# Feed-forward: the hidden chunks turned in 32x32 blocks by VectorE and a trip through device memory instead of by TensorE

## The reference, cut to what matters

```python
D_MODEL = 1024; SEQ = 256; DEPTH = 4
FFN_HIDDEN = -(-8 * D_MODEL // (3 * 256)) * 256        # 2816

def swiglu(h, w_gate, w_up, w_down):
    return (jax.nn.silu(h @ w_gate) * (h @ w_up)) @ w_down

for i in range(DEPTH):
    ...                                                # mixer
    f = swiglu(rms_norm(x, norm_gains[i, 2]), ffn_w_gate[i], ffn_w_up[i], ffn_w_down[i])
    x = x + rms_norm(f, norm_gains[i, 3])
```

## Time and profile before

| | us |
|---|---|
| median of three executions | 1390.9 |
| span of the profiled execution, first to last instruction | 1388.9 |
| TensorE busy in the span | 1368.8 |
| VectorE busy | 996.3 |
| ScalarE busy | 793.3 |
| GpSimd busy | 177.8 |
| DMA queue of SyncE, share of 16 engines' span | 48.4% |
| granted TensorE clock over the span | 1.000 |

### The profile page before, as it was taken

The page is one execution under the profiler, slowest core; times in us unless marked ns, Lnnn a source line. Parts: engine busy times, 40 slices in busy tenths (PEclk is TensorE's granted clock), DMA queues, the critical chain, the costliest instruction groups (busy, mean ns, idle before and its releaser), DMA issues.

```text
span 1388.9 us, 20395 instructions
## 1 busy us (share of the span) xinstructions
PE 1368.8 (99%) x6833; PEld 1117.6 (80%) x6833; DVE 996.3 (72%) x1889; ACT 793.3 (57%) x1556; POOL 177.8 (13%) x323
## 2 busy tenths in 40 slices
PE   7999999999999999999999999999999999999998
PEld 6888888887887888889888888888888888877667
DVE  6978655559566755569766555599888666789976
ACT  6676644547665645548656554467665445675344
POOL 4100000000111000002000000001049992000000
PEclk9999999999999999999999999999999999999999
DMA  8534655555423755553336555545356556353132
GB/s 290 167 113 142 231 181 183 189 187 187 146 96 113 248 181 188 193 181 120 122 96 223 187 194 193 182 141 178 122 175 212 181 182 207 126 182 122 61 121 92
DMA packets 154389, 230.35 MB, mean 166 GB/s; under 512 B 7512, under 2 KB 103328, under 8 KB 154320
## 3 DMA queue, kind: packets, MB, share of 16 engines
q1 hardware_dynamic: 152352, 224.05, 48.4%
q0 software_dynamic: 1968, 5.43, 1.4%
HBM read 228.40 MB, written 1.05 MB: 165 GB/s over the span
## 4 chain that ended last, share of the span: by engine, by line
PE 90%; DVE 6%; ACT 2%; issue 1%; DMA 0%; SPq 0%; DVEq 0%; ACTq 0%
PE ps L2050 23%; PE ps L2052 23%; PE ps L2051 23%; PE ps L2056 3%; PE ps L2064 3%; PE ps L2060 3%; PE ps L2980 1%; DVE w_rest L1348 1%; PE ps L2328 1%; PE ps L2387 1%; DVE x L1411 1%; PE ps L2080 1%; ACT w_head L817 1%; PE ps L2894 1%; PE ps L2316 1%
## 5 line engine op out<-in xcount | busy, mean ns | idle before, releaser
L2050 PE MATMUL ps<-w_head,xt_head 128*128 128x512 f32 (+1 forms) x1200 | 471.4, 393 | 4.3 <-DVE w_rest L1348 2.5
L1348 DVE SCALAR_TENSOR_TENSOR w_rest<-w_raw,gain_t,w_head 128x512 fp32r<-128x512 f32 (+1 forms) x596 | 415.4, 757 | 74.7 <-ACT w_head L817 73.8
L817 ACT ACTIVATE w_head<-w_raw,gain_t 128x512 fp32r<-128x512 f32 (+1 forms) x596 | 375.4, 700 | 154.8 <-PE ps L2052 125.3
L2052 PE MATMUL ps<-w_head,xt_rest 128*128 128x512 f32 (+1 forms) x1200 | 461.1, 384 | 0.0
L2051 PE MATMUL ps<-w_rest,xt_head 128*128 128x512 f32 (+1 forms) x1200 | 460.2, 384 | 0.0
L2050 PEld LDWEIGHTS ps<-w_head,xt_head 128*128 128x128 f32 x1200 | 226.5, 189 | 49.9 <-issue 8.3
L2052 PEld LDWEIGHTS ps<-w_head,xt_rest 128*128 128x128 f32 x1200 | 226.2, 188 | 45.3
L2051 PEld LDWEIGHTS ps<-w_rest,xt_head 128*128 128x128 f32 x1200 | 226.8, 189 | 40.7
L1346 DVE TENSOR_TENSOR w_rest<-w_raw,w_head 128x1024 fp32r<-128x1024 f32 x124 | 153.4, 1275 | 82.2 <-ACT w_head L817 81.7
L817 ACT ACTIVATE w_head<-w_raw 128x1024 fp32r<-128x1024 f32 x124 | 124.7, 1053 | 98.2 <-PE ps L2052 96.8
L2050 PE MATMUL ps<-w_head,ht_head 128*128 128x512 f32 x320 | 124.9, 390 | 0.0
(11 more groups left out here) (493 smaller groups left out, 1543.5 us busy)
## 6 DMA issues: line engine op xcount, KB each, us to landing
w_raw<-in_ffn_w_gate_dram SPq DMA_DIRECT2D x88, 512.0 KB, 3.7
w_raw<-in_ffn_w_up_dram SPq DMA_DIRECT2D x88, 512.0 KB, 4.7
w_raw<-in_ffn_w_down_dram SPq DMA_DIRECT2D x88, 512.0 KB, 4.1
w_raw<-in_a_w_in_dram SPq DMA_DIRECT2D x48, 512.0 KB, 4.7
w_raw<-in_b_w_in_dram SPq DMA_DIRECT2D x24, 512.0 KB, 4.6
w_raw<-in_w_in_dram SPq DMA_DIRECT2D x24, 512.0 KB, 4.4
w_raw<-in_a_w_out_dram SPq DMA_DIRECT2D x16, 512.0 KB, 4.4
w_raw<-in_c_w_in_dram SPq DMA_DIRECT2D x10, 512.0 KB, 4.4
```

Of the source, the lines that this page charges most:

```text
L817: ins = act.activation(w_head[:, s, w], raw(u)[:, w], ACT.Copy, scale=1.0 if by is None else by)
L1348: ins = dve.scalar_tensor_tensor(w_rest[:, s, w], raw(u)[:, w], by, hd, ALU.mult, ALU.subtract)
L2050: pe.matmul(out_, hd, wh, start=first, stop=False)
L2052: return pe.matmul(out_, rt, wh, start=False, stop=last)
```

## The change

Of the eleven chunks of each feed-forward part, chunks 1 to 9 are no longer transposed by TensorE. `hidden` now writes `hid` with the token blocks side by side. VectorE turns all 16 blocks of 32x32 of each 128x128 tile in one instruction (`blocks_turned`) into `hid_blocks`, a part of `q_t`. What remains is to move blocks between the four groups of 32 partitions. SyncE does that with one DMA of 256 KB to a new tensor in device memory (`hidden_out`, 2 KB per partition), and, behind the completion of that, four DMAs of 64 KB back to `hid_there`, a part of `k_t` (`hidden_in`, runs of 512 bytes, 32 partitions each). ScalarE's and VectorE's `hidt` then read `hid_there` in SBUF instead of bank 6. Chunk 0 and chunk 10 are transposed by TensorE as before.

```diff
+BY_DMA = NCH - 2
 ...
+        hid_blocks = q_t[:, 0:2, :].rearrange("p i t -> p (i t)")
+        hid_there = k_t[:, 0:2, :].rearrange("p i t -> p (i t)")
+        hid_way = nc.dram_tensor("hid_way", (P, 2 * TOK), F32).ap()
+        arrived = hid_there.rearrange("p (a g j) -> p g a j", a=4, g=4)
 ...
 # SyncE
+                def hidden_out(c, more=0):
+                    sp.wait_ge(hid_turned, BY_DMA * li + c + more)
+                    sp.dma_start(hid_way[:, :], hid_blocks).then_inc(hid_out, 16)
+
+                def hidden_in(c, more=0):
+                    sp.wait_ge(hid_out, 16 * (BY_DMA * li + c) + more * 16)
+                    for b in range(4):
+                        rows = slice(32 * b, 32 * b + 32)
+                        sp.dma_start(hid_there[rows, :].rearrange("p (a e) -> p a e", a=4),
+                                     hid_way[:, P * b:P * b + P].rearrange("(a i) e -> i a e", a=4)).then_inc(hid_in, 16)
 ...
-                with sp.Fori(0, NCH - 1) as i:
-                    load_gu(u + 2, i * 3, 0, (i + 1) * FCH)
-                    load_gu(u + 3, i * 3, 4, (i + 1) * FCH)
-                    load_down(u + 4, i * 3, i * 2)
+                for i in range(2):
+                    load_gu(u + 2 + 3 * i, 0, 0, (i + 1) * FCH)
+                    load_gu(u + 3 + 3 * i, 0, 4, (i + 1) * FCH)
+                    load_down(u + 4 + 3 * i, 0, 2 * i)
+                with sp.Fori(0, NCH - 3) as i:
+                    load_gu(u + 8, i * 3, 0, (i + 3) * FCH)
+                    hidden_out(1, i)
+                    load_gu(u + 9, i * 3, 4, (i + 3) * FCH)
+                    hidden_in(1, i)
+                    load_down(u + 10, i * 3, i * 2 + 4)
                 u += 2 + 3 * (NCH - 1)
+                hidden_out(BY_DMA)
+                hidden_in(BY_DMA)
                 load_down(u, 0, 2 * (NCH - 1))
 ...
 # ScalarE
-                    act.wait_ge(hidt_ready, f + c + 1 + more)
-                    act.activation(ht_head[:, :, :], ps[:, 6, :].rearrange("p (t c) -> p t c", t=2), ACT.Copy).then_inc(hidt_head, 1)
+                def hidt(c, down_before, more=0):
+                    act.wait_ge(unit_used, down_before + 1 + more * 3)
+                    act.wait_ge(hid_in, 64 * (BY_DMA * n["ffn"] + c) + more * 64)
+                    act.activation(in_order(ht_head), arrived, ACT.Copy).then_inc(hidt_head, 1)
 ...
 # VectorE
-                        last = dve.scalar_tensor_tensor(hid[:, m, :], ps[:, bank + m, FCH:2 * FCH], rstd_x[:, m:m + 1], gate_s[:, m, :], ALU.mult, ALU.mult)
+                        up, gated = (t_.rearrange("p (t c) -> p t c", t=2) for t_ in (ps[:, bank + m, FCH:2 * FCH], gate_s[:, m, :]))
+                        last = dve.scalar_tensor_tensor(hid[:, :, P * m:P * m + P], up, rstd_x[:, m:m + 1], gated, ALU.mult, ALU.mult)
 ...
+                def blocks_turned(c, more=0):
+                    dve.wait_ge(hid_done, f + c + 1 + more)
+                    dve.transpose(hid_blocks.rearrange("p (b g j) -> p g b j", b=4, g=4),
+                                  hid.rearrange("p t (m b i) -> p (t m) b i", m=M, b=4)).then_inc(hid_turned, 1)
 ...
+                    dve.tensor_tensor(in_order(ht_rest), arrived, in_order(ht_head).bitcast(F32), ALU.subtract).then_inc(hidt_rest, 1)
 ...
                 hidden(1, bank=4)
+                blocks_turned(1)
                 rest(u + 2 + RING)
 ...
                     rest(u + 5 + RING, i)
                     hidden(2, i)
+                    blocks_turned(2, i)
                     rest(u + 6 + RING, i)
                     rest(u + 7 + RING, i)
                     hidt(2, i)
 ...
 # TensorE
                 down(u + 4, 0, first=True)
-                turn_hidden(1)
                 with pe.Fori(0, NCH - 3) as i:
+                    pe.wait_ge(hid_done, f + 2 + i)
                     gate_up(u + 5, i)
                     down(u + 7, 1, i)
-                    turn_hidden(2, i)
                 u += 2 + 3 * (NCH - 2)
+                pe.wait_ge(hid_done, f + NCH - 1)
                 gate_up(u)
                 two_last(u + 2)
```

More of the change, by code:

```diff
@@ L196, in build @@
         gate_s = sb("gate_s", [P, M, FCH])
-        hid = sb("hid", [P, M, FCH])
+        hid = sb("hid", [P, 2, TOK])
         ht_head = sb("ht_head", [P, 2, TOK], F32R)
@@ L310, in build, with in_order @@
         masks_raw = flat(sc[:, :, :], len(MASKS) * MAP)
+        hid_blocks = q_t[:, 0:2, :].rearrange("p i t -> p (i t)")
+        hid_there = k_t[:, 0:2, :].rearrange("p i t -> p (i t)")
+        hid_way = nc.dram_tensor("hid_way", (P, 2 * TOK), F32).ap()
+        arrived = hid_there.rearrange("p (a g j) -> p g a j", a=4, g=4)
+        def in_order(t_):
+            return t_.rearrange("p t (m a j) -> p (t m) a j", m=M, a=4)
         def C(name):
@@ L355, in build @@
         hidt_ready = sem("hidt_ready")
+        hid_turned = sem("hid_turned")
+        hid_out = sem("hid_out")
+        hid_in = sem("hid_in")
         hidt_head = sem("hidt_head")
@@ L1113, in silu, with hidt_first @@
                     last.then_inc(silu_done, 1)
-                def hidt(c, more=0):
-                    act.wait_ge(hidt_ready, f + c + 1 + more)
+                def hidt_first():
+                    act.wait_ge(hidt_ready, 2 * n["ffn"] + 1)
                     act.activation(ht_head[:, :, :], ps[:, 6, :].rearrange("p (t c) -> p t c", t=2), ACT.Copy).then_inc(hidt_head, 1)
+                def hidt(c, down_before, more=0):
+                    act.wait_ge(unit_used, down_before + 1 + more * 3)
+                    act.wait_ge(hid_in, 64 * (BY_DMA * n["ffn"] + c) + more * 64)
+                    act.activation(in_order(ht_head), arrived, ACT.Copy).then_inc(hidt_head, 1)
                 head(u + RING)
@@ L1122, in ffn @@
                 head(u + 1 + RING)
-                hidt(0)
+                hidt_first()
                 silu(u + 4, bank=4)
@@ L1127, in ffn @@
                 head(u + 4 + RING)
-                hidt(1)
+                hidt(1, u + 4)
                 with act.Fori(0, NCH - 3) as i:
@@ L1133, in ffn @@
                     head(u + 7 + RING, i)
-                    hidt(2, i)
+                    hidt(2, u + 7, i)
                 v = u + 3 * (NCH - 3)
@@ L1138, in ffn @@
                 head(v + 6 + RING, some=(0, 2))
-                act.wait_ge(hidt_ready, f + NCH)
+                act.wait_ge(hidt_ready, 2 * n["ffn"] + 2)
                 act.activation(LAST_HT[0], ps[:, 6, :].rearrange("p (t c) -> p t c", t=2), ACT.Copy).then_inc(hidt_head, 1)
@@ L2974, in gate_up, with turn_hidden @@
                         last.then_inc(unit_used, 1)
-                def turn_hidden(c, more=0):
-                    pe.wait_ge(hid_done, f + c + 1 + more)
+                def turn_hidden(c):
+                    pe.wait_ge(hid_done, f + c + 1)
                     for t in range(2):
                         for m in range(M):
-                            last = pe.transpose(ps[:, 6, TOK * t + P * m:TOK * t + P * m + P], hid[:, m, P * t:P * t + P], ident)
+                            last = pe.transpose(ps[:, 6, TOK * t + P * m:TOK * t + P * m + P], hid[:, t, P * m:P * m + P], ident)
                     last.then_inc(hidt_ready, 1)
```

6 lines of the change are left out of this document (4 added, 2 removed).

## The result

| | median of runs (us) | span of the profiled run | TensorE busy |
|---|---|---|---|
| before | 1390.8 (1390.6 to 1391.6) | 1388.9 | 1368.8 |
| after | 1410.9 (1409.5 to 1413.4) | 1411.7 | 1364.5 |

The account below looks back on a forecast made before the run. TensorE was taken as the bound, busy 1368.8 of 1388.9 us. Span 1388.9 - 17.6 (transposes) + 1.2 + 4.7 (waits at starts) = 1377.2, median 2.0 above: 1379 us; forecast 1376 to 1383, range 1373 to 1388.

Parts of the forecast that it names:

- what goes: TensorE's stream: nine chunks in each of four feed-forward parts lose their transposes, 36 x 0.49 = 17.6 us.
- the turn: VectorE's turning of blocks after `hidden`: taken as 0.65 us, 0.9 in the fourth part.
- the loop while it is on time: Settled chunks: hidden chunk ready at s+12.9, 3.4 us ahead of `down(c)` at s+16.33, so everything is hidden.
- The chain can also close on itself: Loop from rest through load, `hidden_in`, copy and subtraction to rest: 14.0 us, below 16.33; late chunks catch up 2.3 per round.
- `hidden_in` lands about 5.5 behind the issue: In the closed chain: `hidden_in` lands 5.5 us after the gate-up load's issue, 9.9 after the rest's end.
- the uncrowded loop: Steady loop: gate-up load issued at s+5.4, last `hidden_in` issue at s+7.9, landing at s+11.5.
- rival 3: The closed chain on ScalarE's `hidt` becomes the bound; 17.3 us a round gives about 1424 us; chance 0.09.
- The starts: Before `down(1)` of each part: TensorE waits 0.4 us in three parts, 4.7 in the fourth.
- the mechanism that was named: Fourth part: GpSimd's table work slows VectorE's eight rests to 10.57 us from 5.38; TensorE waits 4.7 us.
- That stays hidden: Second part: VectorE's 1.5 us of other work behind `hidt(1)` costs nothing; chunk 2 has some 2.4 us of room.
- the rule cited there: Fourth part: VectorE instructions with two SBUF inputs contend with GpSimd reading SBUF; new subtraction may take 0.7 us longer.
- if TensorE waits in settled chunks: Stated sign that the prediction is wrong: TensorE idle in settled chunks, where no wait was forecast.

Follow-up runs that it names:

- run 8: Changed kernel with 40 idle TensorE transposes between `down(0)` and `gate_up(2)` of each part: 1406.2 us, 1.0105 of the kernel before, some 17.6 us of padding included.
- run 3: Changed kernel with `hidden_out` ahead of both gate-up loads, in two kernels: `hidden_in` after both loads, 1417.0 us; after the first, 1374.4 us.
- run 4: Changed kernel with the down load behind `hidden_in` issued only once `hidden_in` has landed: 1390.8 us, 0.9999 of the kernel before.
- run 6: Changed kernel without GpSimd's table work in the fourth part (fills instead): 1396.9 us, 1.0048 of the kernel before.
- run 9: Changed kernel in the order `hidden_out`, gate-up load, `hidden_in`, gate-up load, with 20 idle ScalarE copies before chunk 1's copy in each part: 1407.5 us, 1.0119.
- run 2: Changed kernel with `hidden_out` and `hidden_in` issued ahead of both gate-up loads and the down load: 1374.6 us, 0.9882 of the kernel before.
- between: Changed kernel with `hidden_out` ahead of the first gate-up load and `hidden_in` between the two: 1374.4 us, 0.9882 of the kernel before.
- run 7: Changed kernel with the trips of parts 1 to 3 issued by GpSimd on its own queue, part 4 on SyncE's: 1412.8 us, 1.0152 of the kernel before.
- out first: Changed kernel with only `hidden_out` moved ahead of the first gate-up load, `hidden_in` staying after both: 1417.0 us, 1.0179 of the kernel before.
- run 10: Kernel before with 14, 17, 20 and 23 idle ScalarE copies ahead of chunk 1's copy in its four parts: 1415.6 us, 1.0177 of the kernel before.

## Why the prediction was wrong, by its own steps

- **Right: what goes, and the turn.** 0.48 per chunk against 0.49, the turn 0.71 against 0.65, `hid_done` in front of `gate_up(c+1)` without a cost, the copy 0.63 and the subtraction 0.69 in their ranges (1.07 and 0.75 in two rounds of the fourth part, beside GpSimd's work; up to 0.7 longer was allowed for).
- **Right as it was put: the loop while it is on time.** Part 1 of run 8 shows it, counted from the first matmul of `down`, which is s (206.32 in the round shown): write issued at s+2.7 (forecast 2.7), load at s+5.5 (5.4), `hidden_in` at s+6.6 (6.35), copy at s+11.9 (11.5). From first issue to copy that is 5.4, forecast 5.2. Parts 1 and 3 hold 16.32 for eight chunks.
- **The step that failed: in "The chain can also close on itself", the term "`hidden_in` lands about 5.5 behind the issue" of the load.** Call the end of the rest, where `hidden` starts, R (174.20 in the round shown). The load's issue was right, R+4.35 forecast and R+4.4 measured, and so was what follows the landing, 4.1 against 3.9. Between them `hidden_in` was to be there at R+9.9, 5.5 behind that issue, and came at R+12.7, 8.3 behind it. That is 2.8 us, and turns the 14.0 into 16.65 where 16.33 was the limit: not a catch-up of 2.3 per round, but a loss. The term was even below the 6.1 (s+5.4 to s+11.5) that the prediction had for the uncrowded loop. By the prediction's own steps 1.0 of it lies ahead of `hidden_in`'s first issue, because the write took 4.7 instead of 2.9 at most, and 1.8 behind it, 6.3 to the copy instead of 4.6; but run 3 shows that the two legs aren't separate prices. The transfer engines were full in both (0.91 and 1.05). About 0.8 of the read comes from the load behind (run 4).
- **The outcome was on the list, with a small chance.** It is the place and mechanism of rival 3, which had 0.09; its 1424 took 17.3 for a round from the outset, where parts 1 to 3 show 16.8 to 17.1, and 3.7 for their starts, where they lost 1.3 to 2.4.
- **The starts.** Forecast 0.4 three times and 4.7; measured 1.5, 1.3, 2.4 and 6.4. In part 1 `hidden_out` and the load ahead took 6.3 from the load's issue (forecast 5.9), and `hidden_in` 4.5 to the copy (forecast 3.9 to the landing). The fourth has the mechanism that was named (run 6), with 11.1 for eight rests instead of 10.6.
- **"That stays hidden", of VectorE's other work in the second part.** It didn't: it is 1.9 us, not 1.5, and a late chunk pays it in full (run 9). That it made part 2 of run 8 late is argued, not shown.
- **Two agreements that don't carry.** The 0.68 of the subtraction behind the slowed rests says nothing for the rule cited there: GpSimd's 128x512 products had ended 2 us before, and the next rest, with two SBUF inputs, took its usual 2.73 as well. Run 6 does bear the rule out, 11.1 against 5.35. And the Trainium skill, DMA: Bandwidth & Descriptors, § Anatomy of one DMA, gives its fixed 2 us for DMAs issued by GpSimd and without the time for the bytes, where the earlier trace rows have 2.0 for a whole write of 256 KB on SyncE's queue: near, and not the same thing.
- **Not foreseen: the clock.** Behind four of the waits TensorE fell to its lower level.

The ledger of the profiled execution (the slowest of the four) against the kernel without the trip (span 1372.5): waits that can be seen, 28.0 more (the 15 above and three of 0.3 to 0.4, less the one of 0.47); matmuls started 0.4 to 0.6 apart, nearly all in slow stretches, 7.4; delays under 0.2 us each, 3.8. That is 39.2, the whole distance to 1411.7. Less the 16.4 that the transposes gave, it is 22.8. Of the 15 waits 11.5 are the first of the parts and 15.8 the settled chunks, where nothing had been counted.

The forecast's stated test caught it: it is wrong "if TensorE waits in settled chunks". The order of SyncE's five items, which the change left as a given, was worth 36 us: run 2 and the kernel "between" take 1374.6 and 1374.4 and beat both kernels by 16 and 36 us.

## What to carry to other kernels

When a result makes a round trip through memory inside a loop that is already fed by large loads, put the trip ahead of them in the issue order, and price the closed chain by all the bytes in flight over its stretch (in front and behind), not by the trip's own landing. Ask whether the chain when late is longer or shorter than the bound engine's period: shorter, and any lateness is paid once; longer, and it can last to the end of the loop, even if the same loop on time would have run free. A wait of TensorE costs more than itself once the clock falls.

## What the runs showed of the hardware

- A small transfer's time is that of its company. The 256 KB write took 2.0 us in one order and 4.7 (median) in another, a 64 KB read 1.9 and 3.9 on the same queue. In the crowded stretches shown the engines moved 291 and 315 GB/s. The Trainium skill, DMA: Bandwidth & Descriptors, § Specifications, gives about 358 GB/s as the limit of memory for one core; the trace stays 12% below it, with the engines' share at 1.05.
- A load issued later delayed a smaller transfer issued earlier on the same queue, by about 0.8 us in late rounds (5.8 against 6.6, run 4), and one on another queue was not spared (6.1 and 8.2 us in two parts of run 7). The Trainium skill, DMA: Bandwidth & Descriptors, § Queues, rings and completion order, says that a transfer engine takes its queues in turn, packet by packet; run 7 doesn't contradict that, but no row here shows the turns. By the same section of the Trainium skill the descriptors of one queue are taken in order, and a later one may still finish its write before an earlier one; whether that is how the load behind costs 0.8 no run here shows.
- TensorE fell to half clock behind or within single waits of 2.0 to 7.6 us, but not behind others of 2.3 and 2.4 in the trace of the kernel after, nor behind one of 2.8 in run 3 (out first). It came back while working, 7 to 14 matmuls later in run 10, at 0.20 us each.
- The same loop ran in two lasting rhythms, 16.32 and mostly 16.4 to 19.1 us a round (runs 7 and 8), by what it met early in a part.
